# Attention in a four-layer network: probabilities divided, turned, copied and multiplied in two parts, rows 3 and 2 first; three units' values in another bank

## What is computed

```python
scores = q @ k.T * HEAD_DIM ** -0.5       # 512 x 512 a head, masked
m = max(scores); p = exp(scores - m); l = sum(p)
o = (p / l) @ v
```

## Time and profile before

| | |
|---|---|
| median of three runs | 2508.51 us (2506.43 to 2509.03) |
| profiled execution | 2508.29 us, span 2506.6 us |
| mean granted TensorE clock | 0.988 |
| TensorE busy | 2411.5 us, 96% |
| VectorE, ScalarE, GpSimd busy | 1410.4, 1083.7, 125.7 us |
| odd layer's pair steps | about 599 to 785 us |
| units of the mixers | about 1322 to 1416 and 1974 to 2068 us |

### The profile page before, as it was taken

One profiled execution on the slowest core, in us unless ns is written; L12 is line 12 of the kernel. 1 busy time (PEld: TensorE's weight loads), 2 busy tenths in 40 slices (PEclk: granted clock), 3 DMA queues, 4 the chain that ended last, 5 costly groups with the idle time before them and its releaser, 6 DMA issues.

```text
span 2506.6 us, 32833 instructions
## 1 busy us (share of the span) xinstructions
PE 2411.5 (96%) x11748; PEld 1912.8 (76%) x11748; DVE 1410.4 (56%) x2270; ACT 1083.7 (43%) x1673; POOL 125.7 (5%) x115
## 2 busy tenths in 40 slices
PE   8989999999999999999999989999989998999997
PEld 6657888887777888887777668888868766788885
DVE  5887777435765677732547764334353767533434
ACT  4444444326876444422447543233253663432322
POOL 0001000000000000001400010000113001000000
PEclk9999999999999999999999999999999999999999
DMA  4112222232121322222211122323222112232322
GB/s 174 61 42 93 99 94 99 94 101 68 59 67 59 101 92 100 92 101 96 103 60 35 51 72 96 100 94 101 93 100 74 43 35 76 76 101 93 101 93 76
DMA packets 57437, 210.61 MB, mean 84 GB/s; under 512 B 6478, under 2 KB 6880, under 8 KB 56960
## 3 DMA queue, kind: packets, MB, share of 16 engines
q1 hardware_dynamic: 56736, 204.51, 24.3%
q0 software_dynamic: 608, 4.81, 0.5%
HBM read 207.20 MB, written 2.10 MB: 83 GB/s over the span
## 4 chain that ended last, share of the span: by engine, by line
PE 67%; issue 22%; DVE 5%; POOLq 2%; ACT 2%; DVEq 1%; POOL 1%; DMA 0%; SPq 0%; ACTq 0%
PE PS L1150 12%; PE PS L1152 12%; PE PS L1151 12%; PE PS L1178 9%; PE PS L1180 9%; PE PS L1179 9%; PE PS L1209 1%; DVE CONV L1819 1%; DVE RSTD L1758 1%; POOLq L573 1%; PE PS L1264 1%; PE PS L1239 1%; PE PS L1242 1%; POOLq L582 1%; PE PS L1240 1%
## 5 line engine op out<-in xcount | busy, mean ns | idle before, releaser
L1744 DVE TENSOR_TENSOR WL<-RAW,WH 128x1024 fp32r<-128x1024 f32 x376 | 476.2, 1267 | 428.7 <-ACT WH L601 427.4
L1150 PE MATMUL PS<-HH,WH 128*128 128x512 f32 x1792 | 708.3, 395 | 7.0 <-DVE KR L1993 4.5
L1152 PE MATMUL PS<-HH,WL 128*128 128x512 f32 x1792 | 698.8, 390 | 0.0
L1151 PE MATMUL PS<-HL,WH 128*128 128x512 f32 x1792 | 698.6, 390 | 0.0
L601 ACT ACTIVATE WH<-RAW 128x1024 fp32r<-128x1024 f32 x376 | 397.1, 1056 | 696.4 <-PE PS L1180 411.0
L1150 PEld LDWEIGHTS PS<-HH,WH 128*128 128x128 f32 x1792 | 337.0, 188 | 84.4 <-issue 8.0
L1151 PEld LDWEIGHTS PS<-HL,WH 128*128 128x128 f32 x1792 | 337.2, 188 | 71.8 <-issue 3.6
L1152 PEld LDWEIGHTS PS<-HH,WL 128*128 128x128 f32 x1792 | 336.9, 188 | 70.8
L1180 PE MATMUL PS<-MH,WL 128*128 128x512 f32 x864 | 336.1, 389 | 0.0
L1178 PE MATMUL PS<-MH,WH 128*128 128x512 f32 x864 | 336.1, 389 | 0.0
L1179 PE MATMUL PS<-ML,WH 128*128 128x512 f32 x864 | 336.1, 389 | 0.0
(11 more groups left out here) (291 smaller groups left out, 2586.8 us busy)
## 6 DMA issues: line engine op xcount, KB each, us to landing
RAW<-wstream SPq DMA_DIRECT2D x376, 512.0 KB, 3.2
W<-cmp_w POOLq DMA_DIRECT2D x2, 2048.0 KB, 8.3
X<-xt SPq DMA_DIRECT2D x4, 512.0 KB, 6.5
out<-X SPq DMA_DIRECT2D x8, 256.0 KB, 2.0
TAB<-tables SPq DMA_DIRECT2D x1, 1871.5 KB, 13.1
WS<-spatial_w SPq DMA_DIRECT2D x1, 512.0 KB, 8.4
BS<-spatial_b SPq DMA_DIRECT2D x1, 256.0 KB, 9.0
PW<-pool_w POOLq DMA_DIRECT2D x2, 128.0 KB, 2.4
```

Of the source, the lines that this page charges most:

```text
L1150: pe.matmul(PS[:, bank, :], WH[:, b, w], HH[:, k, :], start=(k == 0), stop=False)
L1151: pe.matmul(PS[:, bank, :], WH[:, b, w], HL[:, k, :], start=False, stop=False)
L1152: last = pe.matmul(PS[:, bank, :], WL[:, b, w], HH[:, k, :], start=False, stop=(k == DC - 1))
L1744: dve.tensor_tensor(WL[:, b, :], RAW[:, b, :], WH[:, b, :].bitcast(F32), ALU.subtract).then_inc(w_lo, 1)
```

## The change

`divide`, `turn_p`, `keep_pt` and `values` now work in two parts over both heads instead of head by head. Part 0 is rows 2 and 3 (seven blocks a head, 896 columns), part 1 rows 0 and 1 (three blocks, 384 columns). `divide` waits for four exponentials for part 0 and for all eight for part 1; each part takes one reciprocal of 2 x 2 sums. `keep_pt` makes four copies of 896, 896, 384 and 384 columns. `values` has 4 + 2 matmuls a head instead of 4. In the odd layer the cosine product of the next keys stays ahead of `divide`, and the other two operations go behind the next `split_lo`. In a mixer's `unit` the `split_lo` goes behind `divide`. Units 3 to 5 put their values into bank 1, so tiles 19 to 21 all use bank 0, and the scores of units 4 and 5 no longer wait for `u_acc`; the values themselves do.

```diff
-    return (s + (s >= Z_OG)) % 2
+    return s % 2 if s < Z_OG else 0
...
+        TURNED = ({0: 0, 1: 256, 2: 512, 3: 768}, {0: 1024, 1: 1280})
+        TURNED_PSUM = (slice(0, 896), slice(1024, 1408))
+        TURNED_SBUF = (slice(0, 896), slice(896, 1280))
...
+        def unit_bank(k):
+            return 2 if k < NSA_PAIRS else 1
...
             def keep_pt(u, PT=PT):
-                for e in range(2):
-                    for part, cols in enumerate((slice(0, T), slice(T, 1280))):
-                        act.wait_ge(at_pt, 4 * u + 2 * e + part + 1)
-                        act.activation(PT[:, e, cols], head_banks(e)[:, cols], ACT.Copy).then_inc(at_ptc, 1)
+                for part in range(2):
+                    for e in range(2):
+                        act.wait_ge(at_pt, 4 * u + 2 * part + e + 1)
+                        act.activation(PT[:, e, TURNED_SBUF[part]], head_banks(e)[:, TURNED_PSUM[part]], ACT.Copy)\
+                           .then_inc(at_ptc, 1)
...
             def turn_p(u, PB=PB):
+                for part, rows in enumerate(((2, 3), (0, 1))):
                     for e in range(2):
+                        pe.wait_ge(at_p, 4 * u + 2 * part + e + 1)
+                        for k, at in TURNED[part].items():
+                            for i in rows:
+                                if i >= k:
+                                    last = pe.transpose(head_banks(e)[:, at:at + P],
+                                                        PB[:, e, ROW_AT[i] + k * P:ROW_AT[i] + (k + 1) * P], tab("identity"))
+                                    at += P
+                        last.then_inc(at_pt, 1)
+
+            def values(u, vt, PT=PT, bank=2):
+                for part, rows in enumerate(((2, 3), (0, 1))):
+                    pe.wait_ge(at_ptc, 4 * u + 2 * part + 2)
+                    for k in TURNED[part]:
+                        at = TURNED[part][k] - TURNED_PSUM[part].start + TURNED_SBUF[part].start
+                        cols = slice(max(k, rows[0]) * P, (rows[1] + 1) * P)
+                        for e in range(2):
+                            last = pe.matmul(PS[e * HD:(e + 1) * HD, bank, cols], vt[:, k, e * HD:(e + 1) * HD],
+                                             PT[:, e, at:at + cols.stop - cols.start], start=(part == 0 and k == 0),
+                                             stop=(part == 1 and k == 1))
                 last.then_inc(at_o, 1)
...
-                    if s == Z_OG:
-                        kept(s - 1)
-                    elif s == Z_OG + 1:
-                        pe.wait_ge(v_kept, 2 * l + 2)
-                    elif s >= 2:
-                        kept(s - 2)
+                    if s >= 2:
+                        kept(s - 1 if s >= Z_OG else s - 2)
...
-                    scores(short, full, {2: (u_acc, UNITS * l + k)} | frees)
+                    scores(short, full, ({2: (u_acc, UNITS * l + k)} if k <= NSA_PAIRS else {}) | frees)
...
+                    if k > NSA_PAIRS:
+                        pe.wait_ge(u_acc, UNITS * l + k)
+                    values(UNIT0[l] + k, VTS[:, k // NSA_PAIRS, :, :], PT2, unit_bank(k))
...
             def divide(u, gates=None, PB=PB, SUM=SUM, RCP=RCP):
-                for e in range(2):
-                    dve.wait_ge(at_exp, 8 * u + e + 7)
-                    dve.reciprocal(RCP[:, 4 * e:4 * e + 4], SUM[:, 4 * e:4 * e + 4])
+                for part, rows in enumerate((slice(2, 4), slice(0, 2))):
+                    share, whole = (x[:].rearrange("p (e i) -> p e i", e=2)[:, :, rows] for x in (RCP, SUM))
+                    dve.wait_ge(at_exp, 8 * u + 4 * part + 4)
+                    dve.reciprocal(share, whole)
                     dve.drain()
                     if gates is not None:
-                        dve.tensor_tensor(RCP[:, 4 * e:4 * e + 4], RCP[:, 4 * e:4 * e + 4], gates(e), ALU.mult)
+                        dve.tensor_tensor(share, share, gates(rows), ALU.mult)
                         dve.drain()
+                    for e in range(2):
+                        for i in (rows.start, rows.start + 1):
+                            row = PB[:, e, ROW_AT[i]:ROW_AT[i] + (i + 1) * P]
+                            ins = dve.tensor_scalar(row, row, RCP[:, 4 * e + i:4 * e + i + 1], None, ALU.mult)
+                        ins.then_inc(at_p, 1)
...
                 maxima(j, "dilated")
-                rope(KR[:], 0, j + 1, c - 1)
+                rope_cos(KR[:], 0, j + 1, c - 1)
                 divide(j)
                 split_lo(base + 3 * m, c + 1)
+                rope_sin(KR[:], 0)
                 split_lo(base + 3 * m, c + 2)
...
+                    divide(UNIT0[l] + k, lambda rows: gates[:, :, rows], PB2, SUM2, RCP2)
                     if slot:
                         lo(slot)
-                    divide(UNIT0[l] + k, lambda e: gate(1 + b, jj, e), PB2, SUM2, RCP2)
```

More of the change, by code:

```diff
@@ L1341, in turn_p @@
             def turn_p(u, PB=PB):
-                for e in range(2):
[L1343 to L1355, removed]
-                    for e in range(2):
-                        last = pe.matmul(PS[e * HD:(e + 1) * HD, 2, k * P:T], vt[:, k, e * HD:(e + 1) * HD],
-                                         PT[:, e, COL_AT[k]:COL_AT[k] + (TT - k) * P], start=(k == 0), stop=(k == TT - 1))
+                for part, rows in enumerate(((2, 3), (0, 1))):
+                    for e in range(2):
+                        pe.wait_ge(at_p, 4 * u + 2 * part + e + 1)
[6 more added lines that the diff above has]
+                        last.then_inc(at_pt, 1)
@@ L1694, in mix_layer @@
                 cmp_values(1)
+                pe.wait_ge(v_kept, 2 * l + 2)
                 unit_values(3)
@@ L1975, in divide, with rope_cos, rope_sin @@
             def divide(u, gates=None, PB=PB, SUM=SUM, RCP=RCP):
-                for e in range(2):
-                    dve.wait_ge(at_exp, 8 * u + e + 7)
-                    dve.reciprocal(RCP[:, 4 * e:4 * e + 4], SUM[:, 4 * e:4 * e + 4])
+                for part, rows in enumerate((slice(2, 4), slice(0, 2))):
+                    share, whole = (x[:].rearrange("p (e i) -> p e i", e=2)[:, :, rows] for x in (RCP, SUM))
+                    dve.wait_ge(at_exp, 8 * u + 4 * part + 4)
+                    dve.reciprocal(share, whole)
                     dve.drain()
                     if gates is not None:
-                        dve.tensor_tensor(RCP[:, 4 * e:4 * e + 4], RCP[:, 4 * e:4 * e + 4], gates(e), ALU.mult)
+                        dve.tensor_tensor(share, share, gates(rows), ALU.mult)
                         dve.drain()
[L1983 to L1986, removed]
+                    for e in range(2):
[3 more added lines that the diff above has]
+                        ins.then_inc(at_p, 1)
             base = O_QKV // 2
             def rope(dst, side, j, c):
+                rope_cos(dst, side, j, c)
+                rope_sin(dst, side)
+            def rope_cos(dst, side, j, c):
                 dve.wait_ge(o_raw, 2 * j + side + 1)
                 dve.tensor_tensor(dst, PS[:, c % 2, :], COSR, ALU.mult).then_inc(o_cos, 1)
+            def rope_sin(dst, side):
                 dve.tensor_tensor(RT[:, side, :], RT[:, side, :], SINR, ALU.mult)
@@ L2216, in unit @@
                     maxima(UNIT0[l] + k, "causal", PB2, NEGMAX2, SUM2)
+                    gates = GT[:].rearrange("p i (e n b) -> p e i n b", e=2, n=NSA_PAIRS)[:, :, :, jj, 1 + b]
+                    divide(UNIT0[l] + k, lambda rows: gates[:, :, rows], PB2, SUM2, RCP2)
                     if slot:
                         lo(slot)
-                    divide(UNIT0[l] + k, lambda e: gate(1 + b, jj, e), PB2, SUM2, RCP2)
                 def unit_add(k):
@@ L2225, in unit_add @@
                     if b == 0:
-                        ins = dve.tensor_copy(o, PS[:, 2, :])
+                        ins = dve.tensor_copy(o, PS[:, unit_bank(k), :])
                     else:
-                        ins = dve.tensor_tensor(o, o, PS[:, 2, :], ALU.add)
+                        ins = dve.tensor_tensor(o, o, PS[:, unit_bank(k), :], ALU.add)
                     ins.then_inc(u_acc, 1)
```

8 lines of the change are left out of this document (3 added, 5 removed).

## The result

The changed kernel takes 2488.89 us, the median of four runs (2487.41 to 2489.62), beside 2507.52 for the kernel before in the same comparison (four executions): a ratio of 0.9925, 95% interval 0.9913 to 0.9938, 18.6 us less. Forecast were 2492.0, a range of 2488 to 2500, and 16.3 us.

A forecast was written before the change was run, and what follows sets the result against it. TensorE, busy 96% of the span, was taken as the bound. Odd layer 5.6, mixers 12.4 and values -1.7 sum to 16.3 us off 2508.3, giving 2492.0 us, range 2488 to 2500.

The forecast's parts named there:

- The holes in the mixers: TensorE's idle time around the mixers' transposes: removed whole, 5.6 and 6.1 us, less 0.3 per mixer for longer copies.
- the 20 transposes: A pair's transposes on TensorE, counted as twice a ten of 1.15 us: 2.30 us.
- Unit 4's wait: In each mixer, unit 4's values wait 0.5 us instead of 0.2 for the longer copies: 0.3 taken off.
- The holes in the odd layer: TensorE's idle time around the odd layer's transposes: removed whole, 0.86 us in each of six steps, 5.2 us.
- Every step has 0.8 us or more in hand: Divided rows would be ready on VectorE at least 0.8 us before TensorE wants them, so holes go whole.
- The last odd step: Seventh odd step, followed by TensorE's wait for the low half of its output: 0.45 us gained.
- The clock rival: Low-clock stretch at the last pair's scores: doubled gives 2494, vanished 2490; inside the forecast's 0.65 chance.
- The bank: Mixers: unit 4's scores no longer wait for unit 3's values to leave bank 2, 0.9 us gained per mixer.
- The cut values: Values matmuls cut from 16 to 24 records cost 0.09 us a pair, 1.7 us over 19 pairs.
- VectorE behind: Mixers' unit 2: scores would newly wait 0.25 us a mixer for VectorE to take out unit 1's sum.
- The rival that VectorE cannot keep up: Mixers' units 0 to 2: 2 us a mixer lost, 2496 us; chance 0.2 shared with partly exposed loads.
- The gain given back behind unit 5: Rival: VectorE's reciprocal chain behind the mixers' unit 5 is fixed in time, losing 11 us: 2503 us; chance 0.05.

The follow-up runs named there:

- the parts alone: Changed kernel with VectorE's moves undone (rotary operations and low half ahead of the division again), order by rows kept: 2496.48 us, ratio 0.9955.
- the moves alone: Kernel before, head by head and without the bank change, with only VectorE's two rotary operations and the mixers' low half moved behind the division: 2504.87 us, ratio 0.9988.
- the run without the rotation: Changed kernel with the rotation of the mixers' last keys left out, a one-column fill in its place: 2486.24 us, ratio 0.9917.
- the two runs with the sum first: Changed kernel with unit 1's sum ahead of the last rotation: 2490.09 us; the second also puts low key halves behind the compressed branch's division: 2491.10.

## Why the prediction was right, and where it was not

The time fell by the forecast's sign and nearly its size, 18.6 us against 16.3, inside the range. Taken by its own steps:

**The holes in the mixers** were what the prediction said. From the last projection record ahead of the transposes to the first record behind them, units 0 to 5 of the first mixer gained 0.89, 1.16, 1.26, 1.14, 0.47 and 0.92 us, 5.84 in all, where 5.6 - 0.3 = 5.3 was forecast. The undersized term is the 20 transposes: they take 2.18 in units 0 to 2 and 2.10 in the odd layer, not twice the 1.15 of a ten, 0.12 and 0.20 less a pair; in units 3 and 5 they take 2.28, next to what was counted. In the second mixer the same six places gained 6.33 against 6.1 - 0.3 = 5.8. Unit 4's wait of 0.49 for the copies was sized rightly at 0.5. The run with the parts alone shows that in the mixers the parts do nearly all of it: without the move of the low half the mixers take 0.11 and 0.25 more.

**The holes in the odd layer** came out near the sum, 6.1 us in six steps and 0.7 in the seventh against 5.2 and 0.45, but the step that explained them failed: "Every step has 0.8 us or more in hand, so I remove the holes whole." The count stopped at the division. Behind it on VectorE stands the low half that the next projection reads, which in the kernel before ended 0.05 us before that projection in the first step. The hole had two ends, tied: the front one by the division, the back one by the low half. The parts alone gained nothing there and the moves alone 0.53 a step; both together gained 1.03. The prediction named the rotation as leaving "the front of the division" and saw no price in it; it was the half of the change without which the odd layer gives nothing. That the forecast came true here is luck in this sense: the change held the move that the count did not know it needed. The low half has 0.35 us in hand now, and 1.36 us put in front of it cost the whole gain, 1.1 a step.

**The last odd step**: 0.73 instead of 0.45 less 0.09. The clock rival came to nothing there: the low stretch neither doubled nor vanished. The granted clock is 0.82 over 763 to 766 and 0.62 over 766 to 769, so the 1.2 GHz level held for part of both, after the 2.85 us in which TensorE was idle; before it was 0.73 over 771 to 774 and 0.70 over the next three. Clock lost in six us: 0.56 x 3 = 1.7 us after, 0.57 x 3 = 1.7 before; and from that pair's scores to the stretch behind the eighth step it takes 22.86 us against 22.72.

**The bank**: 0.94 a mixer from unit 3's values to unit 4's scores, forecast 0.9; the kernel without it gave back 0.91 in the first mixer, and in the second 0.9 beside a clock fall of 1.5.

**The cut values** cost nothing: 2.31 us for 16 and for 24 records, 2.34 for 40. Sized at 0.09 a pair, this was 1.7 us too dear, since I took the 0.17 that the columns leave as a price of each pass. At the projection's own pace, 0.23 us for a record of 512 columns, the 2 x 2 x 1280 columns alone are 2.3 us, and nothing is left for the passes. The time stays the same when the records rise from 16 to 40. TensorE: Matmul & The Clock Gate in the Trainium skill (LDWEIGHTS; The mechanism) gives such a load 53 ns and says that it overlaps a matmul in flight only where the row groups differ; by an estimate from that, eight would cost 0.42 us a pair. The runs disagree: 24 further records add 0.03. That section of the Trainium skill also lets loads for a background weight buffer go ahead of matmuls, which the runs do not contradict.

**VectorE behind**: the place and the kind of the wait were right (unit 2's scores), the size was not: shown as 0.58 and 0.77, worth 0.49 and 0.68 by the run without the rotation, forecast 0.25. The rival that VectorE cannot keep up was thus true by a quarter to a third of its 2 us a mixer. Neither order tried freed room there.

**The gain given back behind unit 5** did not happen; the 1.69 us wait moved with the values, for the reason given.

Put together for the first mixer: 5.84 from the holes, 0.94 from the bank, 0 for the values, -0.5 for VectorE: 6.28, measured 6.12. For the second 6.33 + 0.94 - 0.7 = 6.6, measured 6.45. For the odd layer 6.1 + 0.7 - 0.1 = 6.7, against 5.0 by the forecast with its share of the values. The terms that were off lay mostly on one side: holes too small, mainly because the transposes were counted too dear, and 1.7 us for the values that nothing cost, less about 0.7 for VectorE. With the terms as measured the sum is 6.28 + 6.6 + 6.7 = 19.6 us; the stretches themselves give 19.3, and the two profiled executions differ by 19.35, in which the 0.6 at the start and the -0.4 of the clock nearly cancel.

Still open: why the clock falls in unit 2 of the second mixer in three traces (bank undone, and the two runs with the sum first) and not in that of the changed kernel, and why the first 15 us of the program differ by some 2 us between traces.

## What to carry to other kernels

When a wait is removed, look behind the released instruction on its own engine: what it makes next may be needed at the very moment the removed wait ended, and then the gain can be zero, as here, until that comes earlier too. Two releasers that end within 0.05 us show as one in the list of waits; read the end of every input of the next instruction, not only the one named. Where the result of small work must be taken out by another engine before TensorE can go on, issue that small work ahead of a long stretch of TensorE, so that the taking out falls under it: that was worth 1.2 us a mixer, while the two reorderings of the engine that was full gained nothing. And before a difference is put down to an edit, compare the granted clock of the stretch in both traces.

## What the runs showed of the hardware

Cutting float32 matmuls of 64-column weights into more pieces over the same columns was free down to 128 columns: 16, 24 and 40 records in 2.31, 2.31 and 2.34 us. Twenty transposes in one row cost 2.10 us in the odd layer, 0.105 each, where a projection follows, and 2.18 or 2.28 in a mixer, where other small work follows; a ten behind a wait took 1.15, which twice is 0.20 and 0.12 more than the first two. A wait can cost less or more than it shows: 0.52 for a shown 0.58, as the eight score records behind it passed in 0.86 us instead of 1.08, but 1.16 for a shown 0.68 in front of unit 5's scores. And the granted clock of the same stretch differs between traces of nearly the same program: 0.50 over 3 us of the second mixer in one, where it cost 1.5 us, and 1.00 in another.
